# Second mixing stage in another order: branches between the projections, whole levels per step, head norms inside attention, root on VectorE

## What is computed

```python
h = rmsnorm(x, attn_norm[l])
z = h @ w_in[l]
(c_q, c_kv, k_rope, g_q, g_k, g_v, g_lr, g_g, r_q, r_k, r_v, r_g) = jnp.split(z, split_points, axis=-1)
y_a = mla_branch(c_q, c_kv, k_rope, mla_q_norm[l], mla_w_uq[l], mla_kv_norm[l], mla_w_ukv[l],
                 mla_cos, mla_sin)
y_a = head_rmsnorm(y_a, mla_out_norm[l]).reshape(B, S, MLA_HEADS * MLA_V)
y_b = gla_branch(g_q, g_k, g_v, g_lr, g_g, gla_w_gate[l], gla_b_gate[l], gla_out_norm[l])
y_c = retention_branch(r_q, r_k, r_v, r_g, ret_out_norm[l], ret_cos, ret_sin)
x = x + jnp.concatenate([y_a, y_b, y_c], axis=-1) @ w_out[l]
...
x = x + (jax.nn.silu(a) * bv) @ ffn_w_down[l]
```

## Time and profile before

| | us |
|---|---|
| median of 3 runs (3962.5 to 3964.42) | 3962.64 |
| the profiled execution | 3967.78 |
| its span in the trace | 3965.9 |
| TensorE busy | 3683.6 (93%) |
| VectorE busy | 2035.7 (51%) |
| POOL busy | 2001.5 (50%) |
| ScalarE busy | 960.4 (24%) |
| mean granted clock | 0.945 |

### The profile page before, as it was taken

One profiled execution on the slowest core, in us unless ns is written; L12 is line 12 of the kernel. 1 busy time (PEld: TensorE's weight loads), 2 busy tenths in 40 slices (PEclk: granted clock), 3 DMA queues, 4 the chain that ended last, 5 costly groups with the idle time before them and its releaser, 6 DMA issues.

```text
span 3965.9 us, 44443 instructions
## 1 busy us (share of the span) xinstructions
PE 3683.6 (93%) x16816; PEld 2995.4 (76%) x16816; DVE 2035.7 (51%) x3081; ACT 960.4 (24%) x1625; POOL 2001.5 (50%) x1205
## 2 busy tenths in 40 slices
PE   6999989999999999998989997977999988789998
PEld 5888767878888888766878886856788766568877
DVE  5542696455533552696555523354666135456641
ACT  2110255231111110255131101213223012232220
POOL 4666532536666666442436664610566653116664
PEclk9999999999999999998999998976999988789999
DMA  3333461413333333370413332300233231103322
GB/s 115 96 97 95 111 163 33 138 48 96 96 97 97 100 94 98 97 183 27 133 55 95 97 97 86 104 25 14 75 98 98 88 110 61 33 22 96 96 91 85
DMA packets 103502, 350.78 MB, mean 88 GB/s; under 512 B 13936, under 2 KB 14608, under 8 KB 102800
## 3 DMA queue, kind: packets, MB, share of 16 engines
q1 hardware_dynamic: 92080, 320.59, 25.6%
q0 software_dynamic: 5184, 18.88, 2.6%
q10 hardware_dynamic: 6048, 8.66, 0.9%
HBM read 318.45 MB, written 2.10 MB: 81 GB/s over the span
## 4 chain that ended last, share of the span: by engine, by line
PE 65%; DVE 17%; issue 7%; ACT 6%; DMA 1%; POOL 1%; ACTq 1%; DVEq 0%; POOLq 0%
PE banks L532 21%; PE banks L533 20%; PE banks L534 20%; DVE diagonals L854 3%; DVE squares L858 1%; DVE pair L2044 1%; ACT diagonals L823 1%; DMA w_raw<-mid 1%; ACT probs L913 1%; DVE scaled L862 1%; DVE diagonals L850 1%; ACT act_hi L831 1%; ACT squares L826 1%; ACT probs L907 1%; PE banks L1750 1%
## 5 line engine op out<-in xcount | busy, mean ns | idle before, releaser
L568 POOL CAST w_hi<-w_raw 128x1024 fp32r<-128x1024 f32 (+1 forms) x566 | 594.2, 1050 | 1754.6 <-PE banks L534 1620.5
L573 POOL TENSOR_TENSOR w_lo<-w_raw,w_hi 128x1024 fp32r<-128x1024 f32 (+1 forms) x534 | 1297.9, 2431 | 42.7
L532 PE MATMUL banks<-h_hi,w_hi 128*128 128x512 f32 x2944 | 1166.2, 396 | 38.5 <-POOL w_lo L573 7.3
L533 PE MATMUL banks<-h_lo,w_hi 128*128 128x512 f32 x2944 | 1154.7, 392 | 0.0
L534 PE MATMUL banks<-h_hi,w_lo 128*128 128x512 f32 x2944 | 1154.1, 392 | 0.0
L532 PEld LDWEIGHTS banks<-h_hi,w_hi 128*128 128x128 f32 x2944 | 557.9, 189 | 177.0 <-issue 27.1
L534 PEld LDWEIGHTS banks<-h_hi,w_lo 128*128 128x128 f32 x2944 | 557.8, 189 | 118.1
L533 PEld LDWEIGHTS banks<-h_lo,w_hi 128*128 128x128 f32 x2944 | 558.7, 190 | 112.9
L532 PE MATMUL banks<-act_hi,w_hi 128*128 128x512 f32 x1056 | 413.0, 391 | 8.5 <-DVE act_lo L864 8.5
L533 PE MATMUL banks<-act_lo,w_hi 128*128 128x512 f32 x1056 | 412.7, 391 | 0.0
L534 PE MATMUL banks<-act_hi,w_lo 128*128 128x512 f32 x1056 | 412.4, 391 | 0.0
(11 more groups left out here) (366 smaller groups left out, 4465.4 us busy)
## 6 DMA issues: line engine op xcount, KB each, us to landing
w_raw<-gu SPq DMA_DIRECT2D x176, 512.0 KB, 3.4
w_raw<-mid SPq DMA_DIRECT2D x120, 512.0 KB, 3.5
w_raw<-up SPq DMA_DIRECT2D x88, 512.0 KB, 3.5
w_raw<-dn SPq DMA_DIRECT2D x96, 448.0 KB, 3.2
w_raw<-mix SPq DMA_DIRECT2D x64, 512.0 KB, 3.4
w_raw<-dn SPq DMA_DIRECT2D x48, 512.0 KB, 3.5
w_lo<-w_raw POOLq DMA_DIRECT2D x26, 512.0 KB, 5.2
w_raw_third<-mid SPq DMA_DIRECT2D x10, 512.0 KB, 5.5
```

The source lines that it names most:

```text
L532: pe.matmul(out, w_hi, m_hi, start=start, stop=False, skip_group_check=True)
L533: pe.matmul(out, w_hi, m_lo, start=False, stop=False, skip_group_check=True)
L568: g.tensor_copy(wh[:, ch.slot, 0:width], raw_tile(ch, width)).then_inc(Ring.hi[ch.slot], 1)
L573: eng.tensor_tensor(wl[:, ch.slot, 0:width], raw_tile(ch, width), f32(wh[:, ch.slot, 0:width]), ALU.subtract).then_inc(Ring.split[ch.slot], 1)
```

## The change

The second mixing stage is rewritten; what is computed stays the same.

- The first products take x times its gain without the root of the norm (`plain_act`, `plain_low`, as the feed-forward does); the root is multiplied in where VectorE, no longer ScalarE, evicts (`zrows`); values get it as ScalarE's scale. k_rope and the gate input share a chunk: 18 z chunks, not 19. The tables are loaded ahead of chunk 3.
- 5 tiles and the values come first. Nine tiles follow, and after each group of 3 matmuls `beside(g)` (g from 0 to 71) may put something between: retention in 3 steps, its values, the 8 levels each as one step of 4 blocks with one predicated copy, the far blocks in 2 steps, and the norms of c_q and c_kv.
- The head norms of the 4 branch tiles are made between the second projections. Their half of the output product stands between the steps of attention, and so do the norms of the first three heads.
- Attention has two score banks and one output bank.
- `root_on_dve` replaces ScalarE's Sqrt for c_q, c_kv, the branches and the four heads: a shift, a linear step and three iterations, 12 small instructions that each wait for the one before.
- A level's second VectorE operation becomes an Abs on ScalarE; Silu of the gates moves behind the first six evictions of the second projections.

```diff
-FIRST_BLOCK = (0, 4, 7, 9)
+FIRST_BLOCK = (0, 4, 8, 12)
-MIX2_CHUNKS = 19 + 3 + 2 + 8
+MIX2_CHUNKS = 18 + 3 + 2 + 8
...
+    def root_on_dve(v, n, total, width, l, turn):
+        def step(i, ins):
+            ins.then_inc(root_s.sem, 1)
+            v.wait_ge(root_s.sem, root_s(l, ROOT_STEPS * turn + i))
...
+        step(1, v.tensor_scalar(var, total, 1.0 / width, 1e-6, ALU.mult, ALU.add))
+        step(2, v.tensor_scalar(bits, var.bitcast(I32), 1, None, ALU.logical_shift_right))
+        step(3, v.tensor_scalar(bits, bits, -1, ROOT_SEED, ALU.mult, ALU.add))
+        for e in range(3):
+            step(3 * e + 4, v.tensor_tensor(tmp, root, root, ALU.mult))
+            step(3 * e + 5, v.scalar_tensor_tensor(tmp, tmp, -0.5, var, ALU.mult, ALU.mult))
+            step(3 * e + 6, v.scalar_tensor_tensor(root, tmp, 1.5, root, ALU.add, ALU.mult))
...
+    RET = [[(a, a + d) for a in range(T - d)] for d in (0, 1)] + [[(0, 2), (1, 3), (0, 3)]]
+    RET_AT, RET_VALUES_AT, FAR_AT = (2, 6, 10), 14, (64, 69)
+    def level_at(n):
+        return 16 + 6 * n
+    def part2_at(d):
+        return 4 + 2 * d
...
     def mix2_pe(pe, l):
-        norm_pe(pe, attnorm, l)
...
+        for j in range(2):
             tile(j)
+        norm_pe_totals(pe, attnorm, l)
+        tile(2)
+        norm_pe_spread(pe, attnorm, l)
+        tile(3)
...
+        def level_group(lv):
...
             pe.wait_ge(lev_q.sem, lev_q(l, 2 * (lv + 1)))
             for a in range(T):
-                n = lv * T + a
-                pe.wait_ge(lev_at.sem, lev_at(l, n - 1))
                 rows = slice(a * P, (a + 1) * P)
-                key_query(n, lambda r: ke[r, lv % 2, rows], lambda r: qe[r, lv % 2, rows])\
-                    .then_inc(lev_ps.sem, 1)
+                mm = key_query(a, lambda r: ke[r, lv % 2, rows], lambda r: qe[r, lv % 2, rows])
+            mm.then_inc(lev_ps.sem, 1)
...
+        for j in range(5, 14):
+            tile(j, beside)
+        pe.wait_ge(far_at.sem, far_at(l, 2))
+        values(0)
...
+        def beside_attention(s):
+            for d in range(KD):
+                if s in (part2_at(d), part2_at(d) + 1):
+                    for e in range(2):
+                        branch_part(d, 2 * (s - part2_at(d)) + e)
+            for h in range(MH - 1):
+                if s == T * h + 10:
+                    head_totals(h)
+                if s == T * h + 12:
+                    head_spread(h)
+
+        attention_pe(pe, mla, l, scores, XSCORE_BANKS, mla.max, causal_tiles, outputs, mla.y_hi, beside_attention, 1)
...
+        for d in range(4):
+            for k in range(MH - 1):
+                head_part(d, k)
+            if d == 0:
+                head_totals(MH - 1)
+            if d == 2:
+                head_spread(MH - 1)
...
     def mix2_dve(v, l):
...
+        def level_group(lv):
             if lv + 2 < 7:
                 level(lv + 2)
-            for a in range(T):
-                n = lv * T + a
-                v.wait_ge(lev_ps.sem, lev_ps(l, n + 1))
-                v.wait_ge(lev_at.sem, lev_at(l, n))
-                gate(v, 6)
-                v.copy_predicated(pair[:, FIRST_BLOCK[a], :, :],
-                                  lmask[:, lv:lv + 1, :].to_broadcast([P, MH, P]),
-                                  score_banks(n)).then_inc(lev_at.sem, 1)
+            v.wait_ge(lev_ps.sem, lev_ps(l, lv + 1))
...
+            gate(v, 6)
+            v.copy_predicated(pair_blocks(0, T), lmask[:, lv:lv + 1, :].unsqueeze(1).to_broadcast([P, T, MH, P]),
+                              pair_banks(0, T)).then_inc(lev_at.sem, 1)
             if lv + 2 < LEVELS:
                 level_qk(lv + 2)
...
+        for j in range(5, 14):
+            for k in range(KD):
+                beside(KD * (j - 5) + k)
+            evict(j)
...
+        for i in range(4):
+            u_low(i)
+        v.wait_ge(bs_tot.sem, bs_tot(l, 1))
+        root_on_dve(v, 32, bank[4][:, 0:32], 64, l, 2)
+        branch_diagonals(4)
+        branch_diagonals(5)
+        u_low(6)
...
+            def load_with_tables(sp, ch, src, width):
+                for l in range(L):
+                    if ch.n == mix2_chunk(l, 3).n:
+                        tables2(l)
+                load(sp, ch, src, width)
```

877 lines of the change are left out of this document (560 added, 317 removed).

## The result

The changed kernel takes 3873.0 us (median of 4 runs, 3868.1 to 3880.8), the kernel before 3963.5: the ratio is 0.9773, with a 95% interval of 0.9756 to 0.9791. It is 90.5 us faster. The forecast was 3797 with a range of 3750 to 3862, so the sign was right, the time lies 11 us outside the range, and the gain is 55% of the 166 us that were added up. The profiled execution took 3875.1 us.

The account below looks back on a forecast made before the run. In the steps between projections TensorE waits on VectorE or ScalarE; linear attention's bound is a hand-over, not an engine. Layer 1 saves 85.2 us, layer 0 80.4, together 165.6: 3967.8 becomes 3802.2, the median 3797, range 3750 to 3862.

Parts of the forecast that it names:

- the nine tiles: Tiles with retention and linear attention between their products: 88 us a layer, bounds 79 (all covered) and 105 (seven hand-overs).
- POOL's contention: In the nine tiles, POOL's chunk splits slow VectorE operations with two SBUF inputs: 18 us, from a possible 0 to 32.
- layer-1 entry: From the last down projection to layer 1's first product: 0 us, where 15.7 passed before.
- the values: Linear attention's values and hand-over, behind the nine tiles: 8.2 + 0.5 = 8.7 us.
- the wait of 7 ahead of the feed-forward: VectorE's backlog of adds, lows and sums before the FFN's first product: 7 us, bounds 2 and 16.
- what follows attention: Remaining output products 21.7, last head norm 2.0, stall of 1: 24.7 us.
- The second projections: Products with branch totals and spreads 35.2, 14.3 uncovered, 1.5 for the branches' root: 51 us, bounds 44 and 60.
- attention: Heads, branches' output share and three head norms 60.2, plus 6.5 of gaps: 66.7 us, bounds 62.2 and 76.4.
- Layer 1's first projections: Five tiles and the values 48.8, gate product 1.0, norm 2.0: 51.8 us.
- Layer 0's entry: Final norm's scaling stays, ending 13.2 us after the stage's start; with the first low 14.1 us.
- VectorE becomes the bound: Rival: the high bounds hold, 44.7 us more a layer, 3887, half of it 3842; chance 0.18.
- The clock rival: Waits hold TensorE's clock down over the interleaved stretch; gain eaten below 0.61, 3996 us at 0.58; chance 0.04.

Follow-up runs that it names:

- later_and_narrow: Changed kernel with TensorE's c_q and c_kv norm steps later and POOL's split of the nine chunks on 128 of 1024 columns only; 3824.5 us.
- norms_later: Changed kernel with TensorE's totals and spreads of the c_q and c_kv norms 2 to 5 groups later, steps that follow 1 to 4; 3844.6 us, ratio 0.9697.
- later_early_filled: Changed kernel with norm steps later, last branch diagonals early, keys evicted ahead of Silu, and 16 unread products a layer; 3837.5 us, ratio 0.9679.
- later_still: Against norms_later: c_q's totals one group later, c_kv's totals ten, directly ahead of their spread, plus the unread products; 3853.8 us.

## Why the prediction was right in sign and wrong in size

**The step that failed** is the nine tiles: "I take 88; the bounds are 79 (all covered) and 105". It was 109.2 and 110.9. The two sums under it were good: VectorE busy 74.9 against 84 forecast (65.5 free, and about 9.7 of POOL's, not 18), TensorE's 78.5 of work (80.2 us of busy time at a clock of 0.98 in `later_and_narrow`). What failed was to go from two sums to a length. I set the longer sum, added 4 us for hand-overs, and priced TensorE throughout at full clock. In fixed orders the length comes from where a step stands in one order against where its input comes in the other. Four norm steps stood 2 to 5 groups too early. Moving them, in `norms_later`, took away 13.1 of layer 0's 21.2 us and 16.0 of layer 1's 22.9; 4.8 of the 13.1 are the clock. What is left is in part POOL's contention, which is worth 17.7 us in the two layers whether the norms are placed or not. The upper bound of 105 had the mechanism ("1 us at each of seven hand-overs") but not its size: the single waits at these steps were 0.7 to 7.0.

**What could have told it.** This is a reckoning, not shown by a run. VectorE has to go through a level's difference, copy and two inputs (0.68 + 2.36 + 2 x 0.68 = 4.4 us) plus eviction, sum and root between g 28 and 34 and between 40 and 50, while TensorE has 0.677 us a group. Added up group by group for both engines, not over the stretch, the waits of 2.4 to 7 us should be found ahead of time from the rows that the forecast used.

**POOL's contention** was right as a mechanism and too large as a term: 7.3 and 10.5 us in the two layers alone, 10.2 and 7.5 with the norms placed, against 18. The forecast took a chunk to be in work nearly always; POOL worked 31.7 of the 109.2 us. The rule of the Trainium skill ("SBUF — State Buffer", "Who interferes with whom") holds by the rows that it was used for: the copies, with a PSUM source, stayed at 2.47 us beside POOL, while one product with two SBUF inputs (L2268) took 2.82 and one low piece (L751) 2.57, for 0.68 free. One case I had not counted is in the last section.

**Other steps.** The layer-1 entry (0), the values, the wait of 7 ahead of the feed-forward (7.2) and what follows attention (25.7 for 24.7) were right. The second projections (52.7 for 51) and attention (71.4 for 66.7) were 1.7 and 4.7 too short; of attention's, 5.2 are the wait for the third head's root, 2.8 of them POOL's hold on its small steps. Layer 1's first projections are 4.5 longer, as its attention norm's spread waits 2.3 us for VectorE's diagonals and the first products behind it run at half the clock. The four diagonals took 5.8 us beside POOL's splits, for 0.87 in layer 0:

```profile
3167.59 5.77 DVE L739 TENSOR_SCALAR diagonals<-ident,stats 128x128 f32<-128x128 f32 x4
```

Layer 0's entry is 3.2 longer, 2.3 of them since POOL, no longer held back by the tables, splits chunks while VectorE adds the final norm's sums; before, then after:

```profile
2433.17 1.48 DVE L652 TENSOR_TENSOR square_sum<-square_sum,squares 128x512 f32<-128x512 f32 x2
```

```profile
2436.45 3.82 DVE L670 TENSOR_TENSOR square_sum<-square_sum,squares 128x512 f32<-128x512 f32 x2
```

**The rivals.** "VectorE becomes the bound" gave 3842 to 3887 and holds the measured time, but not for its reason: VectorE was idle a third of the stretch. The clock rival did not decide the sign (0.87 in the nine tiles, 0.61 needed), yet it was there at a smaller size in nearly every stretch, 0.81 in the second projections, and my forecast gave it nothing at all. Its ground, "0.57 to 0.58 wherever TensorE waits for a third of the time", was read too strictly: the earlier trace rows also have stretches with 30% and 29% of waiting at 0.66 and 0.86.

The fastest kernel that leaves nothing out is `later_early_filled`, 3837.5 us: 127 below the kernel before in its own set and about 31 below the changed one. Without the unread products it is `norms_later`, 3844.6.

## What to carry to other kernels

When work of two engines is interleaved in orders fixed by hand, add up both engines' time from one meeting point to the next, not over the stretch: a step that stands too early stops its own engine, and then the other one waits for what stands behind it. Leave the supplier room between two steps that wait for one another: `later_still` had none and won nothing. When a wait is taken away, look where it comes back and at the granted clock behind it. And before a difference of a few microseconds between two kernels is put down to the edit, compare them stage by stage and layer by layer: here a stage that no edit had touched took 71.4 us in one layer and 78.5 in the other, as much as some of the effects that were being tested.
